# Experts in an order computed on the chip, rows beyond 128 in small fp32 units

## The chip, the cores and the metric

The kernel runs on one core of a Trainium2 chip. The metric is the device time of one execution in microseconds (us), the median of several runs. TensorE (PE in the profile), VectorE (DVE), ScalarE (ACT), GpSimd (POOL) and the queue of SyncE (SP) are the engines that the text names.

## The reference

One inference step of one decoder layer in fp32 for a prompt of 2048 tokens and 8 sample tokens, so 2056 rows of width 1024: a mixer (mLSTM heads and a chunk MLP), then a mixture of experts, then a gated embedding and a norm. What the change touches is the mixture:

```python
g_sel = jnp.argmax(g_prob, axis=-1)                      # one of 4 groups
top_v, top_i = lax.top_k(e_logits, TOP_K_IN_GROUP)       # two of its 8 experts
weights = g_w * jax.nn.softmax(top_v, axis=-1)
expert_idx = (g_sel[:, None] * EXPERTS_PER_GROUP + top_i).astype(jnp.int32)
# rows of an expert, in blocks of 128:
(jax.nn.silu(xb @ w1_l[e]) * (xb @ w3_l[e])) @ w2_l[e]
```

w1 and w3 are 1024 x 512 and w2 is 512 x 1024 for each of the 32 experts, 6.3 MB together. The 4112 choices are spread unevenly over the experts.

## The kernel before

There are four stages, each a block with a barrier at its end. Stages 1 and 2 are the mixer, tile by tile of 128 tokens. In stage 2 the router runs on each tile and GpSimd scatters each row's number into `list_dram`, where every expert has a region of CAP rows. At the end of stage 2 TensorE sums the experts' counts over all partitions (`POS`, L1421), and VectorE turns them into a table `blk` of the first block and the end block of each expert (L1751 to L1764), with at least one block for each. The list of expert 0 is loaded (L1907), its rows are gathered (L1911), its w1 is loaded by `load_first` and split by ScalarE ahead of the barrier.

Stage 3 is the expert stage (L2009 to L2257). All engines run over the experts 0 to 31 in their order, `all_blocks`, and within an expert over its blocks of 128 rows, read from `blk` into registers. The products are made in fp32r with operands split in two parts: hi is the value as fp32r (a ScalarE copy), lo the difference (a VectorE or GpSimd subtraction), and a product is hi x hi, hi x lo and lo x hi.

- TensorE, `block_of` (L2106): 24 products of 512 columns for w1 into bank H1 and 24 for w3 into H3 (L2113 to L2115), 8 transposes of the next block's rows (L2102) and 4 of `hid` (L2121), and 24 products for w2 into two banks (L2132, L2136).
- ScalarE: tanh of H1 (L2174), the copy of the block before's result into `y_sb` and its store (`y_out`, L2163), the hi copies of hid and of x, and once an expert, `after`: the hi copies of the next expert's w3 and w2 and of the w1 after that.
- VectorE: `up` and `hid` (L2217, L2222), the lo parts of hid and x, and five of the six half matrices of lo weights an expert (L2212). GpSimd makes the sixth, the second half of w1 (L2070), in about twice the time.
- GpSimd also loads the next block's list (L2056) and gathers its rows by indirect DMA (L2061).
- SP: `reload` loads each half matrix of the next expert (1 MB) as soon as the raw buffer is free, which is when the lo part has been made. There are three raw buffers, and 4 slots each of w_hi and w_lo, so that a part can be split while the expert before is still in use. SP also copies 16 blocks of filler into the part of `y_dram` that no block writes (L2033).

After the last block VectorE computes for each token and choice its row in `y_dram` (`choices_rows`, L2230), and the weights of the last stage's gate are loaded and split in the same way. Stage 4 gathers two result rows for each token, adds them to h, and makes the gate, the embedding and the norm, tile by tile.

## Time and profile before

| | us |
|---|---|
| median of 3 runs | 2258.27 |
| lowest and highest | 2257.19, 2259.78 |
| the profiled execution | 2255.27 |
| its span, first to last instruction | 2253.7 |
| mean granted TensorE clock of it | 0.977 |

The rows come from one profiled execution. PE is TensorE's products, PEld its weight loads, which overlap them. Times in the rows of the timeline are from the span's start. A product's duration in a row includes its way through the array; the distance between two starts is what a stream of them costs. A true-fp32 product shows as two records, a product in fp32r as one.

### The profile page before, as it was taken

The numbers are of one execution on the slowest core, as the hardware profiler recorded it, in microseconds if no ns is written. First come the engines' busy times: TensorE is split into PE (matmuls) and PEld (weight loads), VectorE is DVE, ScalarE is ACT, GpSimd is POOL, SyncE is SP. The second block draws the span as 40 slices with busy tenths as digits, with TensorE's granted clock in tenths as the row PEclk, the third lists the DMA queues.
The fourth block names the chain that finished last, engine by engine and source line by source line (L and its number), as shares of the span: only waits on it lengthen the run. The fifth ranks groups of instructions, "written<-read, shape, count | busy, mean of one in ns | idle before, by whom it ended". The sixth has DMA issues, their size and how long they took to land. (4 is left out here: it accounts for less than half of the span.)

```text
span 2253.7 us, 34056 instructions
## 1 busy us (share of the span) xinstructions
PE 2149.3 (95%) x10539; PEld 1773.2 (79%) x10540; DVE 1430.6 (63%) x2866; ACT 971.0 (43%) x1569; POOL 581.7 (26%) x595
## 2 busy tenths in 40 slices
PE   6999999999899999994889999999999999899998
PEld 5878888888788888884778888888888878767775
DVE  5788888888566665564536465665566566846554
ACT  4433344444432222222435465665556465623332
POOL 1121111111244333332121223233332132233332
PEclk9999999999999999996999999999999999999999
DMA  6111110132534333324787677898787778943441
GB/s 231 60 38 66 65 60 37 65 112 92 187 107 136 121 121 117 103 91 147 292 309 256 219 266 289 292 363 289 283 294 260 289 290 305 334 169 125 158 141 49
DMA packets 160333, 407.13 MB, mean 181 GB/s; under 512 B 18835, under 2 KB 22347, under 8 KB 160014
## 3 DMA queue, kind: packets, MB, share of 16 engines
q1 hardware_dynamic: 138518, 337.17, 42.0%
q0 software_dynamic: 14560, 43.11, 5.8%
q10 hardware_dynamic: 7200, 26.22, 2.9%
q8 instruction: 23, 0.38, 0.1%
q14 instruction: 32, 0.26, 0.0%
HBM read 330.12 MB, written 84.82 MB: 184 GB/s over the span
## 5 line engine op out<-in xcount | busy, mean ns | idle before, releaser
L234 PE MATMUL bank<-w_hi,mix_x 128*128 128x512 f32 x816 | 333.3, 408 | 9.9 <-DMA mix_x<-xT_dram 4.0
L236 PE MATMUL bank<-w_hi,mix_x 128*128 128x512 f32 x816 | 323.8, 397 | 0.0
L235 PE MATMUL bank<-w_lo,mix_x 128*128 128x512 f32 x816 | 322.9, 396 | 0.0
L2113 PE MATMUL bank<-w_hi,x_hi 128*128 128x512 f32 x784 | 307.6, 392 | 8.1 <-POOL w_lo L2070 4.6
L2212 DVE TENSOR_TENSOR w_lo<-raw,w_hi 128x2048 fp32r<-128x2048 f32 x130 | 292.6, 2311 | 34.8 <-ACT w_hi L2149 34.7
L2115 PE MATMUL bank<-w_hi,x_lo 128*128 128x512 f32 x784 | 307.1, 392 | 0.0
L2114 PE MATMUL bank<-w_lo,x_hi 128*128 128x512 f32 x784 | 307.1, 392 | 0.0
L2149 ACT ACTIVATE w_hi<-raw 128x2048 fp32r<-128x2048 f32 x130 | 238.8, 1925 | 4.8 <-DMA raw<-in_w 4.8
L2070 POOL TENSOR_TENSOR w_lo<-shared,w_hi 128x2048 fp32r<-128x2048 f32 x31 | 157.2, 5071 | 231.7 <-DMA shared<-hn_dram,entry 131.9
L234 PEld LDWEIGHTS bank<-w_hi,mix_x 128*128 128x128 f32 x816 | 156.7, 192 | 42.0 <-issue 5.1
L236 PEld LDWEIGHTS bank<-w_hi,mix_x 128*128 128x128 f32 x816 | 156.3, 192 | 34.7
L235 PEld LDWEIGHTS bank<-w_lo,mix_x 128*128 128x128 f32 x816 | 156.7, 192 | 29.9
L2113 PEld LDWEIGHTS bank<-w_hi,x_hi 128*128 128x128 f32 x784 | 148.5, 189 | 39.9 <-POOL w_lo L2070 5.0
L2115 PEld LDWEIGHTS bank<-w_hi,x_lo 128*128 128x128 f32 x784 | 148.4, 189 | 31.0
L2114 PEld LDWEIGHTS bank<-w_lo,x_hi 128*128 128x128 f32 x784 | 148.5, 189 | 30.9
L248 POOL TENSOR_SCALAR stat<-stat 128x4 f32<-128x4 f32 (+3 forms) x67 | 13.4, 200 | 514.2 <-ACT junk L716 271.2
L2061 POOL DMA_INDIRECT shared<-hn_dram,entry x49 | 68.2, 1392 | 282.9 <-DMA entry<-list_dram 139.3
L2149 ACT ACTIVATE hidT_hi<-bank 128x128 fp32r<-128x128 f32 x98 | 37.6, 384 | 226.3 <-PE bank L2121 226.3
L2217 DVE SCALAR_TENSOR_TENSOR up<-tanh_h,bank 128x512 f32<-128x512 f32 x49 | 33.5, 684 | 157.4 <-ACT tanh_h L2174 157.4
L2132 PE MATMUL bank<-w_hi,hidT_hi 128*128 128x512 f32 x392 | 126.6, 404 | 0.0
L2132 PE MATMUL bank<-w_lo,hidT_hi 128*128 128x512 f32 x392 | 122.3, 393 | 0.0
L2149 ACT ACTIVATE w_hi<-shared 128x2048 fp32r<-128x2048 f32 x64 | 119.7, 1921 | 4.7 <-DMA shared<-in_w 3.9
(316 smaller groups left out, 4222.1 us busy)
## 6 DMA issues: line engine op xcount, KB each, us to landing
raw<-in_w SPq DMA_DIRECT2D x128, 1024.0 KB, 8.5
shared<-in_w SPq DMA_DIRECT2D x64, 1024.0 KB, 8.6
y_dram<-y_sb ACTq DMA_DIRECT2D x50, 512.0 KB, 6.9
xT_dram<-mix_x SPq DMA_DIRECT2D x34, 512.0 KB, 3.5
mix_x<-xT_dram SPq DMA_DIRECT2D x34, 512.0 KB, 4.5
shared<-in_w_in SPq DMA_DIRECT2D x24, 512.0 KB, 6.5
small<-in_x_prompt SPq DMA_DIRECT2D x16, 512.0 KB
xr_sb<-in_x_prompt SPq DMA_DIRECT2D x16, 512.0 KB
```

The lines of the kernel that those rows point to most:

```text
L234: pe.matmul(bank[:, :], x_hi[:, k, :], wh[:, k, :], start=(k == 0), stop=False)
L235: pe.matmul(bank[:, :], x_hi[:, k, :], wl[:, k, :], start=False, stop=False)
L236: ins = pe.matmul(bank[:, :], x_lo[:, k, :], wh[:, k, :], start=False, stop=(k == KD - 1))
L2061: pool.indirect_dma_start(out=rows_in[:, :], out_offset=None, in_=hn_dram[0:NT * P + NS, :], in_offset=bass.IndirectOffsetOnAxis(ap=entry[ ...
L2070: pool.tensor_tensor(w_lo[slot(j, 0)][:, cols], raw[0][:, cols], w_hi[slot(j, 0)][:, cols].bitcast(F32), ALU.subtract).then_inc(w1_lo, 1)
L2113: pe.matmul(bank[:, :], x_hi[:, k, :], wh[:, k, :], start=(k == 0), stop=False)
L2114: pe.matmul(bank[:, :], x_hi[:, k, :], wl[:, k, :], start=False, stop=False)
L2115: ins = pe.matmul(bank[:, :], x_lo[:, k, :], wh[:, k, :], start=False, stop=(k == KD - 1))
L2132: pe.matmul(Y[n][:, :], hidT_hi[:, k, :], col(w, k, n), start=(k == 0 and w is wh), stop=False)
L2149: return act.activation(out, in_, ACT.Copy)
L2212: dve.tensor_tensor(w_lo[slot(j, m)][:, cols], raw[m][:, cols], w_hi[slot(j, m)][:, cols].bitcast(F32), ALU.subtract).then_inc(w1_lo if is ...
L2217: STT(up[:, :], tanh_h[:, :], 1.0, H1[:, :], ALU.add, ALU.mult).then_inc(up_done, 1)
```

## The change

**Order.** At the end of stage 2 VectorE computes, beyond the counts, for each expert the number of units of 32 rows that it has beyond its first 128 rows, and a place in a sequence of steps: one with no unit, then pairs of one expert with units and one without, and at the end what is left. The table `blk` has three rows: first unit, end unit and expert of each step. Three bounds in `ends_of` say where the pairs begin, where they end and which is the last step. List, rows and w1 of the first expert can be fetched only when its number is known (after 30 of the 43 small steps), and w1 is split behind the barrier.

**Steps.** Every step runs the first 128 rows of its expert as before. An expert with more rows has these in units of 32 rows. A unit of the expert of step s + 1 runs in step s, from the raw weights of step s + 1 in true fp32, which have been loaded but not yet used up: 32 products of 256 columns (w1 and w3 side by side) and 16 for w2, four neighbours of which write the four quarters of the partitions. Between the two groups, each unit runs the first half of w2's product of step s.

**Buffers.** w_hi and w_lo have 3 slots in place of 4. TensorE waits for the next step's split w1 between the two halves of w2's product. The next w1 is loaded when the units are done (`tails_done`).

**Other parts.** The filler of `y_dram` is 12 copies of 368 rows in stage 1, in place of 16 copies of 128 rows in stage 3. `choices_rows` is in the last step, ahead of `up`, with another formula for the row. The result rows of a unit are stored as 32 rows.

The core of the diff:

```diff
+                            TS(blk[:, 0, 0:NE], POS, float(TAIL - 1 - P), None, ALU.add).then_inc(rank_steps, 1)
...
+                            TT(placed[0], at.unsqueeze(1).to_broadcast([P, TABLE, NE]), number[:, :].unsqueeze(2).to_broadcast([P, TABLE, NE]), ALU.is_equal).then_inc(rank_steps, 1)
...
                             sp_.wait_ge(log_mm, NTILE)
-                            load_first(1)
+                            sp_.wait_ge(rank_steps, 30)
+                            expert = sp_.value_load(blk[0:1, 2, 0:1], min_val=0, max_val=NE - 1)
+                            for c in range(2):
+                                load_first(expert, c)
...
-                            for c in range(2):
-                                act.wait_ge(raw_loaded[0][c], 16)
-                                copy(w_hi[0][:, c * RH:(c + 1) * RH], shared[:, c * RH:(c + 1) * RH]).then_inc(hi_ready, 1)
...
+                def each_step(eng, ends, step):
+                    pairs, tails, last = ends
+                    step(0, False)
+                    with eng.Fori(1, pairs) as s:
+                        step(s, False)
+                    with eng.Fori(pairs, tails, 2) as s:
+                        step(s, True)
+                        step(s + 1, False)
+                    with eng.Fori(tails, last) as s:
+                        step(s, True)
+                    step(last, False, True)
...
+                        def step(s, more):
+                            x1 = expert_at(sp_, s + 1)
+                            wait_lo(sp_, s, 1, 1)
+                            load(x1, 1, raw_loaded[1])
+                            wait_lo(sp_, s, 2, 1)
+                            load(x1, 2, raw_loaded[2])
+                            x2 = expert_at(sp_, s + 2) if more else None
+                            sp_.wait_ge(tails_done, s + 1)
...
+                        def down(n, k):
+                            wh, wl, cols = w_down(w_hi), w_down(w_lo), slice(n * 512, (n + 1) * 512)
+                            begun = pe.matmul(Y[n][:, :], hidT_hi[:, k, :], wh[:, k, cols], start=(k == 0), stop=False)
+                            pe.matmul(Y[n][:, :], hidT_hi[:, k, :], wl[:, k, cols], start=False, stop=False)
+                            return begun, pe.matmul(Y[n][:, :], hidT_lo[:, k, :], wh[:, k, cols], start=False, stop=(k == KF - 1))
...
+                        def tail(i, s):
+                            for m in range(2):
+                                for c in range(2):
+                                    pe.wait_ge(*raw_in(s + 1, m, c))
+                            pe.wait_ge(t_x_in, i + 1)
+                            w13 = raw13[:, :].rearrange("p (m k n) -> p m k n", m=2, k=KD)
+                            for k in range(KD):
+                                for q in range(TILES):
+                                    ins = pe.matmul(UP_T[q * TAIL:(q + 1) * TAIL, :].rearrange("p (m n) -> p m n", m=2), xT_t[:, k, :],
+                                                    w13[:, :, k, q * P:(q + 1) * P], start=(k == 0), stop=(k == KD - 1))
+                            ins.then_inc(t_up_mm, 1)
+                            ready_down(s)
+                            for k in range(KF):
+                                down(0, k)
+                            pe.wait_ge(t_rows, 16 * i + 32)
+                            pe.wait_ge(t_hid, i + 1)
+                            pe.transpose(HID_T, hid_t[:, :], ident[:, :]).then_inc(t_hid_tp, 1)
+                            tail_transposes()
+                            for c in range(2):
+                                pe.wait_ge(*raw_in(s + 1, 2, c))
+                            pe.wait_ge(t_y_in, i + 1)
+                            pe.wait_ge(t_hidT_in, i + 1)
...
+                            for k in range(KF):
+                                for q in range(TILES):
+                                    ins = pe.matmul(DOWN_T[q * TAIL:(q + 1) * TAIL, :], hidT_t[:, k * TAIL:(k + 1) * TAIL],
+                                                    w2[:, k, q * width:(q + 1) * width], start=(k == 0), stop=(k == KF - 1))
+                            ins.then_inc(t_down_mm, 1)
...
+                            if tailed:
+                                with pe.Fori(first, end) as i:
+                                    tail(i, s)
+                            else:
+                                ready_down(s)
                                 for k in range(KF):
-                                    ins = pe.matmul(Y[n][:, :], hidT_lo[:, k, :], col(wh, k, n), start=False, stop=(k == KF - 1))
-                                ins.then_inc(done, 1)
+                                    down(0, k)
+                            if not last:
+                                for c in range(2):
+                                    wait_lo(pe, s + 1, 0, c)
+                            for k in range(KF):
+                                begun, ended = down(1, k)
+                                if k == 0:
+                                    begun.then_inc(tails_done, 1)
```

ScalarE's and VectorE's order in a step: x copies and lo, then w3, then (ScalarE) the result of the step before, w2, its store, tanh, the next step's w1, hid, the next x, and the units.

## Rows read from the trace of the kernel before

**Rows 1.** The page: busy time of TensorE, share of the span, instructions.

```profile
PE 2149.3 (95%) x10539; PEld 1773.2 (79%) x10540; DVE 1430.6 (63%) x2866; ACT 971.0 (43%) x1569; POOL 581.7 (26%) x595
```

**Rows 2.** Windows: the mixer, then parts and whole of the expert stage.

```profile
core 0: us, PE busy (x) PEld busy (x) DVE busy (x) ACT busy (x) POOL busy (x), PEclk, DMA share, GB/s
0.00:1050.00 1050.00, 994.91 (x5293) 847.39 (x5294) 734.08 (x2198) 374.65 (x839) 238.71 (x313) 0.97 0.30 100
1061.00:1166.00 105.00, 92.30 (x398) 75.19 (x399) 52.24 (x48) 48.10 (x51) 20.34 (x11) 0.91 0.87 326
1166.00:1966.00 800.00, 793.34 (x3720) 653.25 (x3718) 481.04 (x461) 461.99 (x489) 230.96 (x117) 1.00 0.79 287
1061.00:1966.00 905.00, 885.64 (x4116) 728.45 (x4116) 533.28 (x509) 510.08 (x539) 251.29 (x128) 0.99 0.80 291
```

**Rows 3.** Lines: first w1/w3 product, last w2 product (count, ns, first and last start).

```profile
L2113 PE MATMUL bank<-w_hi,x_hi x784: 389/389/792, 1061.4 to 1957.3; 128*128 128x512 f32 x196
L2136 PE MATMUL bank<-w_hi,hidT_lo x392: 388/389/390, 1080.5 to 1965.6; 128*128 128x512 f32 x196
```

**Rows 4.** Timeline of TensorE (start, duration, count): products and transposes.

```profile
1086.65 0.39 PE L2114 MATMUL bank<-w_lo,x_hi 128*128 128x512 f32 x1
1086.88 0.39 PE L2115 MATMUL bank<-w_hi,x_lo 128*128 128x512 f32 x1
...
1094.13 0.60 PE L2102 MATMUL bank<-ident,shared 128*128 128x128 f32 x4
...
1238.35 0.62 PE L2132 MATMUL bank<-w_hi,hidT_hi 128*128 128x512 f32 x2
1238.80 0.63 PE L2132 MATMUL bank<-w_lo,hidT_hi 128*128 128x512 f32 x2
```

**Rows 5.** Timeline of VectorE: `hid` of two neighbouring blocks.

```profile
1236.14 0.75 DVE L2222 SCALAR_TENSOR_TENSOR hid<-up,bank 128x128 f32<-128x128 f32 x2 [1.44 <-PE bank L2115]
1254.05 0.75 DVE L2222 SCALAR_TENSOR_TENSOR hid<-up,bank 128x128 f32<-128x128 f32 x2 [4.19 <-PE bank L2115]
```

**Rows 6.** Waits in the expert stage: TensorE for GpSimd's half of w1.

```profile
PE bank L2113 <- POOL w_lo L2070: 4.6, 1, 4.6
```

**Rows 7.** True-fp32 products: records of L2399, then L2399 and L1360 in the timeline.

```profile
L2399 PE MATMUL bank<-shared,hz x136: 590/592/1192, 1973.1 to 2232.3; 128*128 128x512 f32 x128, 128*8 128x512 f32 x8
...
2074.80 3.59 PE L2399 MATMUL bank<-shared,hz 128*128 128x512 f32 x8
...
1034.06 1.13 PE L1360 MATMUL bank<-small,shared 128*8 128x36 f32 x16 [0.37 <-ACT shared L1426]
```

**Rows 8.** Timeline from the last rank product to the expert stage.

```profile
1041.20 0.64 PE L1421 MATMUL bank<-seen,ones 128*128 128x32 f32 x2 [1.43 <-DVE idx_last L1665]
1041.87 0.19 DVE L1751 TENSOR_SCALAR blk<-bank 128x32 int32<-128x32 f32 x1 [0.73 <-PE bank L1421]
1042.10 0.18 DVE L1753 TENSOR_SCALAR blk<-blk 128x32 int32<-128x32 int32 x1
...
1045.99 0.63 POOL L1907 DMA_DIRECT2D entry<-list_dram  x1 [1.70 <-DMA list_dram<-tok_last,idx_last]
1049.22 1.05 POOL L1911 DMA_INDIRECT shared<-hn_dram,entry  x1 [2.61 <-DMA entry<-list_dram]
...
1055.43 4.49 DVE L2212 TENSOR_TENSOR w_lo<-shared,w_hi 128x2048 fp32r<-128x2048 f32 x2 [12.05 <-PEq L1198]
```

**Rows 9.** Timeline of the last block's end: row numbers (DVE), y store (ACT queue).

```profile
1962.94 1.29 DVE L2235 TENSOR_TENSOR hot<-rowbase,ecap 128x1088 f32<-128x1088 f32 x1
1966.77 0.34 ACTq L2170 DMA_DIRECT2D y_dram<-y_sb  x1
```

**Rows 10.** Timeline: ScalarE's and VectorE's splits of 4 half matrices, GpSimd's of one.

```profile
1256.87 7.34 ACT L2149 ACTIVATE w_hi<-raw 128x2048 fp32r<-128x2048 f32 x4
1258.83 8.90 DVE L2212 TENSOR_TENSOR w_lo<-raw,w_hi 128x2048 fp32r<-128x2048 f32 x4 [1.00 <-ACT w_hi L2149]
L2070 POOL TENSOR_TENSOR w_lo<-shared,w_hi x31: 4557/4611/6407, 1100.3 to 1939.7; 128x2048 fp32r<-128x2048 f32 x31
```

**Rows 11.** DMA issues to landing, us: weights, filler, and list and gather (min/median/max).

```profile
raw<-in_w SPq DMA_DIRECT2D x128, 1024.0 KB, 8.5
y_dram<-hn_dram SPq DMA_DIRECT2D x16, 512.0 KB, 15.0
DMA to landing us min/median/max: 2.4/4.8/15.1
DMA to landing us min/median/max: 4.1/6.7/15.1
```

More of the change, by code:

```diff
@@ L2090, in _, with shift @@
-                        hold(pool, rows_loaded, 16)
-                        with pool.Fori(0, NE // SLOTS - 1) as quad:
-                            for j in range(SLOTS):
-                                expert(quad * SLOTS + j, j)
-                        for j in range(SLOTS):
-                            expert(NE - SLOTS + j, j)
+                        def shift(bits):
+                            return nc.s_assert_within(bits, 0, 17, skip_runtime_bounds_check_because="none or all of the bits, by a flag of 0 or 1")
@@ new lines, in step @@
+                        def step(s, tailed, last=False, apart=2):
+                            if last:
+                                return
+                            if tailed:
+                                mine, after = expert_at(pool, s + 1), expert_at(pool, s + apart)
+                                first, end = span(pool, s + 1)
+                            gather(s + 1)
+                            if tailed:
+                                with pool.Fori(first, end) as i:
+                                    left = nc.s_assert_within(end - i - 1, 0, 127, skip_runtime_bounds_check_because="i runs from first to end - 1")
+                                    more = (left + 127) >> 7
+                                    here = nc.s_assert_within(mine * CAP + (i + 1 - first) * TAIL + P, P, (NE + 1) * CAP,
+                                                              skip_runtime_bounds_check_because="a unit is one of its expert's")
+                                    gather_tail(i + 1, (here >> shift(17 - 17 * more)) + ((after * CAP + P) >> shift(17 * more)))
+                            load_list(s + 2)
+                            split_w1(s + 1)
@@ L2187, in _ @@
+                            if tailed:
+                                with act.Fori(first, end) as i:
+                                    tail(i, s)
+                        act.sem_inc(t_stored, 16)
+                        act.sem_inc(t_y_in, 1)
                         act.sem_inc(y_stored, 16)
+                        ends = bounds(act)
                         x_halves(0)
-                        split(0, 0, 1)
-                        split(0, 0, 2)
-                        all_blocks(act, block_of, after)
@@ L2192, in _ @@
-                        total = count_all(act)
-                        y_out(total)
-                        act.wait_ge(y_stored, total * 16 + 32)
+                        split(0, 0)
+                        each_step(act, ends, step)
+                        split(ends[2] + 1, 1)
+                        y_halves(ends[2] + 1)
+                        y_out(ends[2] + 1)
+                        total = entry_of(act, 1, ends[2], MAXT, 1)
+                        act.wait_ge(t_stored, total * 16 + 16)
@@ L2263, in program @@
+                        ends = bounds(dve)
+                        split(0, 0, (0,))
+                        split(0, 0, (1,), w1_lo)
+                        each_step(dve, ends, step)
+                        split(ends[2] + 1, 1, signal=gate_lo)
         with ExitStack() as late:
```

572 lines of the change are left out of this document (350 added, 222 removed).

## The prediction

> **What bounds the kernel now.** I read the page's busy line first: TensorE is busy 95% of the span [rows 1], so what is worth anything is TensorE time, or idle time of TensorE. The windows over the expert stage come next: it runs from the first w1 product at 1061.4 us to the last w2 product at about 1966.0 us, 904.6 us [rows 2, 3], with the DMA engines 80% busy and 291 GB/s moved. The form counts give the work: 784 products of L2113 are 49 blocks of 16 [rows 3]. In the timeline fp32r products start 0.226 us apart (0.227 in w2) and four transposes take 0.60 us [rows 4]: 48 x 0.226 + 12 x 0.1 + 24 x 0.227 = 17.5 us, and the distance between two blocks' `hid` is 17.91 us [rows 5]. So 49 blocks are 877 us and the stage has 27.5 us of stalls and half clock; the first 105 us hold most of them (clock 0.91, PE busy 92.3) [rows 2], one being a 4.6 us wait for the half of w1 that GpSimd splits [rows 6].
>
> **What the change does to the work.** Evaluating the reference's router on its inputs gives the rows of each expert: 4112 choices, 32 experts with 73 to 194 rows, which round up to the 49 blocks of the trace. 17 experts have more than 128 rows and their rests make 25 units of 32 (ten experts with one, six with two, one with three). That gives 32 steps: steps 0 and 1 without a unit, then 12 pairs (units, none), steps 26 to 30 with units, step 31 without. The terms:
>
> (a) *17 blocks gone*: 17 x 17.9 = -304.3 us on the bounding engine. The old stalls, -27.5, go too and are put in anew below.
>
> (b) *25 units*. One is 32 + 16 = 48 true-fp32 products of 256 columns, each writing 32 partitions, with four neighbours going to the four different quarters of the partitions. No operation like this is in the trace. The nearest: a true-fp32 product shows as two records (136 of L2399 for 68 products), and eight records of 512 columns in 3.59 us start 0.43 us apart [rows 7], so one 256-column record streams for about 0.214 us and a product for 0.43. The cheapest fp32 records, 36 columns with 8 stationary columns, start 0.06 us apart [rows 7]; that is the floor of issue. If four quarters work side by side, a record costs the larger of 0.214/4 and 0.06 us: 96 x 0.06 = 5.8 us a unit. If nothing overlaps it is 48 x 0.43 = 20.6 us. These are the two bounds, and they are far apart. To either come 9 small transposes at 0.1 [rows 4] and four handovers (units to down, to transposes, to down, back) for which I put 0.2 each, since a block of two or three handovers loses 0.4 us in all (17.9 against 17.5): +1.7. I take the lower end, U = 7.5 us, because the products of one group write different partitions and read nothing of each other, but it is the choice on which all hangs: 25 x 7.5 = +187.5.
>
> The Trainium skill, "TensorE: Matmul & The Clock Gate" (Part 3, row/col tiling), speaks for it: small-M products in distinct column groups run concurrently, three of them measured 2.38 times faster than in sequence. By 2.38 a unit's products would take 20.6/2.38 = 8.7 us and the sum would be some 70 us higher, an estimate from that page; no run here shows it yet.
>
> (c) *The first half of w2's product is repeated by each unit* as a filler behind the unit's w1/w3 product (it restarts the accumulation, so only the last counts): 8 units beyond an expert's first x 12 x 0.228 = +21.9. The filler, 2.7 us, covers the chain tanh, two small VectorE operations, about 1.5 us; without it that chain would cost 25 x 1.5.
>
> (d) *The start*. After the last rank product at 1041.2 VectorE does 8 small steps; the entry list is fetched at 1046.0, the gather issued at 1049.2, the stage entered at 1055.4, the first product starts at 1061.4 [rows 8, 3]. Now the first expert must be known before its list or its w1 is fetched: 30 steps, of them 14 dependent rounds at 0.22 and 10 others at 0.1 (4.1 us), three over 1152 elements at 1.3 (the nearest, 1088 elements, takes 1.29 [rows 9]), so 1050.3 instead of 1043.4, and with a register load 1051.4 for the list: everything up to the stage's entry 5.5 us later. w1's split, until now done ahead of the barrier, comes behind it: x copies, ACT 2 x 1.9, VectorE 2 x 2.3, x_lo 1.3 bring the first product to about 1072.4: +11 (between +7 and +15).
>
> (e) *New stalls*. The 4 slots for split weights become 3, with one raw buffer for each matrix, and TensorE now waits for the next step's w1 between the two halves of w2's product. In a step that follows units, counted from the last unit's end: ScalarE copies and stores y (0.8), splits w3 (3.7, to 4.5), copies Y (5.6), splits w2 (9.3), issues, tanh (10.4), splits w1 (14.1), GpSimd's half ends 4.6 to 6.4 us later at 18.8 to 20.6 [rows 10]. TensorE has 2.7 + 10.9 + 1.6 + 2.7 = 17.9 us of work until it asks. Stall about 2 us in 12 steps, 24 us; in steps with units the same split hides behind the units. Steps 0 and 1: 4. In 17 steps with units the products ask for raw w3 at 12.5 us, its load goes out when VectorE has freed the buffer at about 3.8 and takes 8.5 [rows 11]: about 1 us each, 17. The row numbers of the choices (4.4 us on VectorE, until now behind the last block, beside the y store [rows 9]) stand in the last step ahead of `up`: 3.5. Half clock at the start as now: 8 (a clock of 0.91 over the first 105 us [rows 2] is 19 us at 1.2 GHz, some 9 lost). Sum +56.5 (20 to 100).
>
> (f) *At nothing*: 12 copies of 1.5 MB in the mixer's loop on SP's queue, in place of 16 of 0.5 MB that stood in the first expert stretch with 15.0 us to landing [rows 11]. Behind each, the next load of x is issued a tile later, and that part moves few bytes (100 GB/s, 30% [rows 2]). If the cover failed it would be up to 12 x 8 us. The second batch of dependent rank steps (to about 1057) ends before the stage is entered. The gather of units: list 4.8, issue 1, landing 6.7 [rows 11], behind at least one unit with its filler; only the expert with three units waits, 2 us. The block's end still waits for the last y store, and the stage after it is unchanged.
>
> Sum: -304.3 - 27.5 + 187.5 + 21.9 + 11 + 56.5 = -54.9 us. The profiled execution took 2255.3 (span 2253.7), the median is 2258.3; I set the difference against the median: **2203 us**.
>
> In general the result is 2258.3 - 242.4 + 25 U: it is no gain at U = 9.7, that is when one of the 48 products costs 0.167 us.
>
> **Rivals.** *Order (slower).* A product's two records go to the same quarter. If records start strictly in program order, the second has to wait out the first, and only the second of one product and the first of the next overlap: 0.218 us a product, 48 x 0.218 + 1.7 = 12.1 us a unit, 25 x 12.1 = 302.5, total +60: **2318**. It decides from 0.167 us a product on. For it: all neighbouring products here start in order and none passes another; two records a product [rows 7]. Against: nothing in these rows has two quarters in it. The same page of the Trainium skill (Part 3, what overlaps) states that MATMULs are monotone in start and end, strict FIFO, and this is what it would do here; the trace agrees as far as it goes, with starts in order 0.43 us apart.
>
> *No overlap at all (slower).* 48 x 0.43 + 1.7 = 22.3 us a unit: +315, **2573**. For it: no product of the trace overlaps another's streaming.
>
> *Transfers.* Units read the raw weights, so their buffers stay occupied and the DMA engines idle in them. The stage moves 32 x 6.3 MB of weights, 20 MB of gathers and 20 of y, 241 MB in the 839 us that I forecast, 288 GB/s, about what it moves now, but in fewer stretches; the best stretch of rows 2 is 326 GB/s at 87%. If w3 and w2 land 3 us after they are wanted in each of the 17 steps with units, the gain is nearly gone: **2253**. Against: pairs give the queues some 46 us for 14.8 MB.
>
> *Not what it says*: a wrong count of units or empty steps would show in the counts; 3 steps too many would be +54, 2257.
>
> **Chances.** Forecast 0.46; order 0.28; transfers 0.10; no overlap 0.10; count 0.02; better than forecast by over 25 us, if stalls vanish, 0.04. A measurement of this kernel can tell about 0.2%, 4.5 us, from no change. Faster 0.53 (forecast, better, part of transfers), same 0.07, slower 0.40. The range from 2180 to 2335 takes in the forecast with its bounds, transfers and order, and leaves out the rest. The forecast's own range is 2180 to 2240.
>
> **What would show it.** The unit's w1/w3 line: 64 records a unit, 3.8 us if four work side by side, 7 if two, 13.7 if none; w2's half of that. 25 executions of tanh on 128 columns, 32 on 512. The first product near 1072. PE idle on the GpSimd split line in every other step, about 2 us. Idle of PE ahead of the unit's product on a DMA of raw weights shows the transfers. The clock in the stage stays at 2.4 GHz (granted 1.00 in the window from 1166 to 1966 [rows 2]); if it were granted half in units, a unit would double. The prediction is wrong above all if a unit's product costs more than 0.167 us.

## The result: about half a per cent slower, where 2.4% faster was forecast

| | us |
|---|---|
| before, median of 8 runs | 2260.23 (2257.19 to 2267.26) |
| after, median of 8 runs | 2275.39 (2270.69 to 2279.43) |
| ratio after/before | 1.006, 95% interval 1.0044 to 1.0075 |
| the profiled execution of after, its span | 2279.43, 2277.8 |
| forecast | 2203, range 2180 to 2335 |

The sign is wrong. The profiled execution is the longest of the eight, 4 us over their median. The page of after, busy line and four of the costliest groups (busy, mean ns, idle time before and what ended it):

```profile
PE 2070.6 (91%) x11832; PEld 1641.3 (72%) x11833; DVE 1449.4 (64%) x2831; ACT 954.0 (42%) x1547; POOL 616.6 (27%) x612
...
L2426 DVE TENSOR_TENSOR w_lo<-raw,w_hi 128x2048 fp32r<-128x2048 f32 x99 | 276.1, 2817 | 123.5 <-ACT w_hi L2327 123.4
...
L2255 PE MATMUL bank<-raw,xT_t 128*32 128x256 f32 x1600 | 116.6, 456 | 54.2 <-DMA raw<-in_w 54.2
L2426 DVE TENSOR_TENSOR w_lo<-shared,w_hi 128x2048 fp32r<-128x2048 f32 x66 | 148.3, 2288 | 26.0 <-ACT w_hi L2327 24.4
L2236 PE MATMUL bank<-w_hi,hidT_hi 128*128 128x512 f32 x288 | 122.1, 424 | 36.1 <-DVE hidT_lo L2470 19.0
```

TensorE lost 79 us of work against [rows 1], as the change promises, and the time went up all the same: from 95% busy it fell to 91%. The lines of the first and the last product of the expert stage, and windows over the stage and over one step of it (columns as in [rows 2]):

```profile
L2284 PE MATMUL bank<-w_hi,x_pair x512: 389/389/795, 1080.7 to 1973.9; 128*128 128x512 f32 x171
L2238 PE MATMUL bank<-w_hi,hidT_lo x288: 387/393/628, 1104.9 to 1989.2; 128*128 128x512 f32 x144
```

```profile
core 0: us, PE busy (x) PEld busy (x) DVE busy (x) ACT busy (x) POOL busy (x), PEclk, DMA share, GB/s
1081.00:1989.00 908.00, 803.30 (x5408) 594.40 (x5408) 542.35 (x440) 490.84 (x515) 284.64 (x143) 0.96 0.75 265
1645.00:1661.00 16.00, 12.80 (x62) 10.36 (x60) 11.61 (x10) 10.28 (x10) 7.47 (x3) 1.00 1.02 351
1661.00:1666.00 5.00, 4.78 (x60) 2.69 (x64) 2.50 (x1) 0.00 (x0) 3.22 (x2) 0.66 0.97 359
1666.00:1672.00 6.00, 6.00 (x65) 3.91 (x57) 1.84 (x4) 0.94 (x3) 0.59 (x1) 1.00 0.15 60
```

The stage takes 908.8 us (1080.7 to 1989.5) against 904.6 before [rows 2, 3]. It holds 105 us in which TensorE is not busy, against 19 before, and a clock of 0.96 against 0.99. What ended TensorE's waits in it (us in total, times, longest), where before had the 4.6 us of [rows 6], 13.7 us for gathers and 3.5 us for `x_lo`:

```profile
PE bank L2255 <- DMA raw<-in_w: 54.2, 17, 4.7
PE bank L2224 <- issue: 25.3, 1, 25.3
PE bank L2236 <- DVE hidT_lo L2470: 19.0, 15, 1.3
PE bank L2236 <- DVE w_lo L2426: 17.1, 13, 1.4
```

The 25.3 us lie ahead of the stage. The other three are new, and the largest is a transfer (each load of `in_w` is a half matrix of weights). Step 20, which has one unit, in TensorE's timeline:

```profile
1657.32 0.49 PE L2301 MATMUL bank<-ident,hid 128*128 128x128 f32 x3
1661.22 5.35 PE L2255 MATMUL bank<-raw,xT_t 128*32 128x256 f32 x64 [3.41 <-DMA raw<-in_w]
1666.50 0.50 PE L2236 MATMUL bank<-w_hi,hidT_hi 128*128 128x512 f32 x1
...
1669.60 0.68 PE L2230 MATMUL bank<-ident,rows_t 32*128 32x32 f32 x8
1670.21 1.93 PE L2273 MATMUL bank<-shared,hidT_t 128*32 128x256 f32 x32
```

TensorE waits 3.41 us for the raw w3 of the next expert, which the unit reads. Then its product takes 5.35 us, in a window in which the granted clock is 0.66 [the windows above]: the level falls to 1.2 GHz during it, behind the wait, and is back at 2.4 GHz from 1666. The DMA engines are the other half of the picture: 1.02 busy at 351 GB/s up to 1661, then 0.15 at 60 GB/s while the unit holds the raw buffers and nothing may be loaded.

**Where the forecast's error lies.** Against its own base (2255.3) the forecast is 2200.4 and the profiled execution is 2279.4, 79 us more. A step is taken from its first w1 product (L2284) to that of the next:

| | forecast, us | measured, us | sum of the difference |
|---|---|---|---|
| first product of the stage | 1072.4 | 1080.7 | +8.3 |
| step 0 | 27.9 | 31.4 | +3.5 |
| 13 steps without units | 19.9 | 21.5 | +20.5 |
| 10 steps with one unit | 26.4 | 29.8 | +34 |
| 6 with two, 1 with three | 36.6, 46.9 | 37.7, 47.3 | +7 |
| the last step | 21.4 | 26.5 | +5 |
| behind the stage | 287.7 | 288.3 | +0.6 |

### The profile page after: what moved, and what is told of

Read it like the earlier page. It is cut to its first block and busy times, and to the rows that moved or that the text cites. A ratio compares the mean times of both kernels' runs of the same rounds, so it can differ in the third digit from the quotient of the medians.

```text
span 2277.8 us, 36186 instructions
## 1 busy us (share of the span) xinstructions
PE 2070.6 (91%) x11832; PEld 1641.3 (72%) x11833; DVE 1449.4 (64%) x2831; ACT 954.0 (42%) x1547; POOL 616.6 (27%) x612
## 5 line engine op out<-in xcount | busy, mean ns | idle before, releaser
L2426 DVE TENSOR_TENSOR w_lo<-raw,w_hi 128x2048 fp32r<-128x2048 f32 x99 | 276.1, 2817 | 123.5 <-ACT w_hi L2327 123.4
L249 PE MATMUL bank<-w_hi,mix_x 128*128 128x512 f32 x816 | 334.1, 409 | 10.2 <-DVE w_lo L232 4.3
L2284 PE MATMUL bank<-w_hi,x_pair 128*128 128x512 f32 x512 | 202.4, 395 | 13.3 <-DVE x_pair L2418 8.7
L2179 POOL TENSOR_TENSOR w_lo<-raw,w_hi 128x2048 fp32r<-128x2048 f32 x31 | 141.3, 4557 | 259.9 <-ACT w_hi L2327 259.8
L2285 PE MATMUL bank<-w_lo,x_pair 128*128 128x512 f32 x512 | 200.3, 391 | 0.0
L2286 PE MATMUL bank<-w_hi,x_pair 128*128 128x512 f32 x512 | 200.2, 391 | 0.0
L2255 PE MATMUL bank<-raw,xT_t 128*32 128x256 f32 x1600 | 116.6, 456 | 54.2 <-DMA raw<-in_w 54.2
L2426 DVE TENSOR_TENSOR w_lo<-shared,w_hi 128x2048 fp32r<-128x2048 f32 x66 | 148.3, 2288 | 26.0 <-ACT w_hi L2327 24.4
L2255 PEld LDWEIGHTS bank<-raw,xT_t 128*32 128x32 f32 x1600 | 60.8, 130 | 104.3 <-issue 83.1
L2284 PEld LDWEIGHTS bank<-w_hi,x_pair 128*128 128x128 f32 x512 | 96.7, 189 | 39.9 <-DVE w_lo L2426 11.0
L2641 PE MATMUL bank<-w_hi,hT_hi 128*128 128x512 f32 x272 | 113.8, 418 | 2.0 <-DVE hT_lo L2714 2.0
L2238 PE MATMUL bank<-w_hi,hidT_lo 128*128 128x512 f32 x288 | 114.8, 399 | 0.0
## 6 DMA issues: line engine op xcount, KB each, us to landing
shared<-in_w SPq DMA_DIRECT2D x66, 1024.0 KB, 10.2
```

The lines of the kernel that those rows point to most:

```text
L249: pe.matmul(bank[:, :], x_hi[:, k, :], wh[:, k, :], start=(k == 0), stop=False)
L2179: pool.tensor_tensor(w_lo[0][:, cols], raw_of(s, 0)[:, cols], w_hi[0][:, cols].bitcast(F32), ALU.subtract).then_inc(w1_lo, 1)
L2255: ins = pe.matmul(UP_T[q * TAIL:(q + 1) * TAIL, :].rearrange("p (m n) -> p m n", m=2), xT_t[:, k, :], w13[:, :, k, q * P:(q + 1) * P], sta ...
L2284: pe.matmul(bank[:, :], x_hi[:, k, :], wh[:, k, :], start=(k == 0), stop=False)
L2285: pe.matmul(bank[:, :], x_hi[:, k, :], wl[:, k, :], start=False, stop=False)
L2286: ins = pe.matmul(bank[:, :], x_lo[:, k, :], wh[:, k, :], start=False, stop=(k == KD - 1))
```

## The experiments

Edits are made to the kernel after. Ratios are against before on the same chip, whose median there was 2259.0 to 2261.5 us. "Step with one unit" and the like are means over steps 1 to 30 of the profiled execution.

**The control** is the kernel after, unchanged.

> The changed kernel as it is, to have its time beside the experiments on one chip. All theories: 2275 us within 5, TensorE's idle time ahead of the units' w1/w3 products about 54 us in 17 waits on raw weights, and these products 5.3 us in the steps where the clock fell, 3.7 where it did not.

2270.6 us, ratio 1.0049 (1.003 to 1.0067). On this chip the wait for raw w3 was 49.8 us in 17 times, the step with one unit 29.1 us. `a1_filled`, `b4_w3_half` and `b1_ahead` ran on the same chip and are read against this.

**Is it the idle time that costs the clock?** `a1_filled` puts twelve products of w2's first half, which the unit repeats anyway, ahead of the wait for raw w3.

```diff
                             if tailed:
+                                ready_down(s)
+                                for k in range(KF):
+                                    down(0, k)
                                 with pe.Fori(first, end) as i:
                                     tail(i, s)
```

> The changed kernel with 12 products that nobody needs (w2's first half, made again later) ahead of the wait for the raw weights in each of the 17 steps with units: 17 x 2.74 = 46.6 us of added work. Theory 1, the weights land late and the idle time costs a second time since the clock falls to 1.2 GHz behind it: the added products stand in the wait, 0.5 us of each wait is left, the clock stays up, 14 x 1.65 = 23 us are saved: about 2252 us, faster than the changed kernel although it does more. Theory 2, only the wait counts and the clock falls for another reason, such as the small products themselves: no change, 2275. Theory 3, TensorE's own work is what the raw weights' buffers wait for, so that all later loads shift by the added work: +47, 2322.

2269.7 us, ratio 1.0037 (1.0023 to 1.0051). Its wait rows, and its unit in step 20:

```profile
PE bank L2236 <- DVE hidT_lo L2473: 40.5, 32, 1.3
```

```profile
1653.04 0.39 PE L2238 MATMUL bank<-w_hi,hidT_lo 128*128 128x512 f32 x1
1653.36 3.66 PE L2255 MATMUL bank<-raw,xT_t 128*32 128x256 f32 x64
```

17 x 2.74 = 46.6 us of work were added and the time did not change, as the second theory had it; the clock did what the first one said. The unit starts at +16.8 us in the step instead of +15.9, without a wait, and takes 3.66 us instead of 5.35. No step with units has a stretch at 1.2 GHz any more (37.5 us of them in the control, 54.6 in after's profile), and the busy time of L2255 is 91.3 us instead of 107.9 in the control and 116.6 in after's profile. So the fall of the clock comes from TensorE standing still ahead of the unit, and its price was 25 us in after's profiled execution and 17 in the control's. It doesn't follow each wait: 14 of the 17 waits had one in after and 10 in the control, with none behind a wait of 3.54 us and one behind 2.15 us. What decides between them is open. The gain was eaten by the filler, which itself has to wait for `hidT_lo` in 17 more steps (40.5 us in 32 times against 19.0 in 15), and by its own length: 46.6 + 21.5 against 49.3 of the wait and 17 of the clock.

**Is the wait one for bandwidth?** `b4_w3_half` loads only the first half of each half of w3 (0.5 MB instead of 1 MB).

```diff
-                        def load(x, m, sems):
+                        def load(x, m, sems, part=1):
...
-                            load(x1, 1, raw_loaded[1])
+                            load(x1, 1, raw_loaded[1], 2)
```

> The changed kernel with each step's load of w3 cut to half its bytes (1 MB in place of 2 MB; the other half of w3 keeps the values of an expert before, so the outputs are not the reference's). Theory 1, bandwidth: the queues are busy without a gap from the release of w1 to the landing of w3, so 3 us of transfer less take away the wait of 3.2 us (54 us) and the low clock behind it (23 us): 2200 us, or a little less. Theory 2, the load is issued late, since it waits for VectorE's lo parts, and takes its latency whatever its size: a latency of 8.9 us falls by about 1 us, 17 us in all: 2258.

2208.5 us, ratio 0.9763 (0.9747 to 0.978). Waits, and the first 13 us of step 20 with the unit's product behind them:

```profile
PE bank L2255 <- DMA raw<-in_w: 7.5, 9, 2.4
```

```profile
1604.60:1617.60 13.00, 12.53 (x61) 10.13 (x59) 8.71 (x8) 9.23 (x9) 4.89 (x3) 1.00 1.02 350
1617.60:1621.40 3.80, 3.75 (x65) 2.22 (x66) 3.70 (x2) 1.06 (x4) 3.65 (x2) 1.00 1.00 385
```

The same rate, 350 GB/s at full share, over 13 us instead of 16: 1 MB less is 3 us less, which is 350 GB/s again. The unit starts 0.5 us after TensorE gets to it, and its clock is 1.00. The median is 62 us under the control's, the profiled execution 56 (2209.8 against 2266.0): 42 of them are the wait (49.8 to 7.5) and some 17 the clock (37.5 us at half in the steps with units, now 3.6), while other steps gave a few us back. So the wait is one for bandwidth, and it brings the clock's fall with it.

**Use the repeated products as the cover, and repeat them no more.** `b1_ahead` has w2's first half once, ahead of the units, and takes it out of `tail`.

```diff
                             ins.then_inc(t_up_mm, 1)
-                            ready_down(s)
-                            for k in range(KF):
-                                down(0, k)
                             pe.wait_ge(t_rows, 16 * i + 32)
...
                             if tailed:
+                                ready_down(s)
+                                for k in range(KF):
+                                    down(0, k)
                                 with pe.Fori(first, end) as i:
```

> The changed kernel with w2's first half made once, ahead of the units (so in the wait for the raw weights), and not again in each unit. Theory 1: 8 x 2.74 = 22 us of repeated products go, 17 x 2.74 = 46 us of the wait are used, the clock stays up (-23), and the chain of tanh, up and hid lies open in each unit, 25 x 1.6 = +40: 2224 us. Rival: the open chain leaves TensorE idle in each unit so that the clock falls there, 25 units with a product of 1.65 us more: 2265. If the wait is not covered (theory 3, loads shift with TensorE's work): 2290.

2232.5 us, ratio 0.987 (0.9853 to 0.9886): faster than both kernels. Waits:

```profile
PE bank L2236 <- DVE hidT_lo L2470: 40.4, 32, 1.3
PE bank L2260 <- DVE up L2433: 28.3, 25, 1.1
```

The wait for raw w3 and the half clock are gone from the steps with units (27.2 us with one, 29.1 in the control). In their place stand the wait for `hidT_lo` and the chain from tanh to the unit's `hid` (a part of the tile `up`), 1.1 us a unit, which the repeated products had covered.

**The steps without units.** TensorE there waits for `hidT_lo` (1.3 us) and for the next w1's lo half (1.3 us). `a2_late_wait` asks for the latter, and gives the signal that frees the raw buffers, at the last product of w2's second half instead of the first.

```diff
-                            if not last:
-                                for c in range(2):
-                                    wait_lo(pe, s + 1, 0, c)
+                            at_k = 0 if tailed or last else KF - 1
                             for k in range(KF):
+                                if not last and k == at_k:
+                                    for c in range(2):
+                                        wait_lo(pe, s + 1, 0, c)
                                 begun, ended = down(1, k)
-                                if k == 0:
+                                if k == at_k:
                                     begun.then_inc(tails_done, 1)
```

> The changed kernel, in steps without units alone: the wait for the next step's split w1, and the signal that lets SP load over it, stand before the last of w2's products in place of the first of its second half. 9 products, 2.0 us, come ahead of the wait, which is 1.4 us in 13 steps. Theory 1, TensorE's wait is on the way and its time is free to take: 13 x 1.4 = 18 us less than the changed kernel, 2252. Theory 2, the same signal starts ScalarE's copy of the result and the next load, both now behind the same VectorE operation plus some of the products, and the next step loses what this one gains: 2270, no change.

2279.1 us, ratio 1.0092 (1.0067 to 1.0116): slower. The steps without units fell from 21.5 to 20.1 us, as the edit should bring, and those with one unit rose from 29.8 to 31.1:

```profile
PE bank L2255 <- DMA raw<-in_w: 71.9, 17, 6.2
```

The next w1's load goes out later and stands in front of w3's. What a step without units gains, the pair's next step gives back in the wait for transfers, and more through the clock (71 us at 1.2 GHz). In the kernel after, the pair is bound by its transfers, not by either step's own work.

`a3_hi_first` runs the eight products with the hi part of `hidT` first and the four with the lo part last, in steps without units.

```diff
+                        def down_hi_first(s):
+                            wh, wl, cols = w_down(w_hi), w_down(w_lo), slice(0, 512)
+                            if not first_step(s):
+                                pe.wait_ge(y_in, 2 * s)
+                            for c in range(2):
+                                wait_lo(pe, s, 2, c)
+                            for part, ks in enumerate(K_OF):
+                                pe.wait_ge(hidT_hi_ready, 2 * s + part + 1)
+                                for k in range(*ks):
+                                    pe.matmul(Y[0][:, :], hidT_hi[:, k, :], wh[:, k, cols], start=(k == 0), stop=False)
+                                    pe.matmul(Y[0][:, :], hidT_hi[:, k, :], wl[:, k, cols], start=False, stop=False)
+                            pe.wait_ge(hidT_lo_ready, 2 * s + 2)
+                            for k in range(KF):
+                                pe.matmul(Y[0][:, :], hidT_lo[:, k, :], wh[:, k, cols], start=False, stop=(k == KF - 1))
...
                             else:
-                                ready_down(s)
-                                for k in range(KF):
-                                    down(0, k)
+                                down_hi_first(s)
```

> The changed kernel, in steps without units alone: w2's first half begins with the 8 products that need only hid's hi part, as before the change, and the 4 with its lo part follow, so that the wait for VectorE's lo part (19.0 us in 15 steps) is covered. Theory 1, the wait is on the way: -19, 2251 us. Theory 2, the wait behind it in the same step, for VectorE's split of the next w1, ends at a time that TensorE does not set, and grows by what the first loses: 2270, no change, and that wait rises from 18 to about 37 us.

2260.9 us, ratio 1.0003 (0.9991 to 1.0015). Waits:

```profile
PE bank L2270 <- DMA raw<-in_w: 44.9, 17, 4.5
PE bank L2236 <- DVE w_lo L2439: 34.9, 14, 3.5
```

The wait for `hidT_lo` is gone, and the wait for w1's lo half took its whole time: 17.1 to 34.9 us. Steps without units became no shorter (22.2 against 21.5). The median is still 14 us under after's and 10 under the control's, each on another chip, and no trace explains that. Against after's profile the wait for w3 is shorter and so are step 0 and the last step, some 2 us each, but that was after's longest execution. Here the profiled execution is the longest of ten, 2266.6, and the control's is the shortest of six, 2266.0: these two are equal. What takes 10 us off the median is open.

**Does alternating carry anything?** `b2_order` makes one pair and puts the other steps without units in a row, then those with units.

```diff
-                            TT(at_step[:, 2:3], at_step[:, 1:2], at_step[:, 0:1], ALU.min).then_inc(rank_steps, 1)
+                            TS(at_step[:, 2:3], at_step[:, 1:2], 0.0, 1.0, ALU.mult, ALU.add).then_inc(rank_steps, 1)
```

> The changed kernel with one pair in place of twelve: steps without units first, 14 in a row, then the experts with units in a row. Theory 1, alternating carries the gain, since steps without units are bound by transfers (7.3 MB a step at 350 to 400 GB/s is 18 to 21 us, and the single buffers leave gaps): each step without units takes 2 us more, +28, 2298 us. Theory 2, alternating is worth nothing or costs: a step behind a step without units has all engines ahead (21.2 us as step 1, against 21.8 in the pairs), and the steps with units in a row take 28.8 and 36.0 us for one and two units, against 29.3 and 37.0 in the pairs: -15, 2255.

2263.0 us, ratio 1.0021 (1.0006 to 1.0037): not slower than the alternating order. The wait for raw w3 is 45.4 us in 17 times, in a row or not. A step with a unit leads to its own wait, whatever comes ahead of it; the likely reason is that the load of w3 that it waits for is issued within it, which no run tests by itself.

**Does the overlap of the quarters depend on neighbours?** `b3_q_outer` exchanges the two loops of a unit's products, so that all of one quarter's come in a row.

```diff
-                            for k in range(KD):
-                                for q in range(TILES):
+                            for q in range(TILES):
+                                for k in range(KD):
                                     ins = pe.matmul(UP_T
```

> The changed kernel with the two loops of a unit's products exchanged: all products of one quarter of the partitions, then the next quarter. The work and its result are the same. Theory 1, quarters run side by side only where neighbours in the program go to different quarters, and products start in program order: 64 records at 0.216 us are 13.8 us in place of 3.7, and 6.9 in place of 1.9 for w2, so 25 x 15.1 = 377 us more, 2648 us. Theory 2, the array has a queue for each quarter and takes them out of order: no change, 2270.

2532.4 us, ratio 1.1211 (1.1178 to 1.1245). In the timeline:

```profile
1650.31 11.50 PE L2255 MATMUL bank<-raw,xT_t 128*32 128x256 f32 x64 [3.12 <-DMA raw<-in_w]
1684.10 4.59 PE L2273 MATMUL bank<-shared,hidT_t 128*32 128x256 f32 x32
```

11.50 and 4.59 us against 3.65 and 1.93: (7.85 + 2.66) x 25 = 263 us, near the difference of the medians, 2532 - 2275 = 257 (two executions, on another chip). The starts of the 64 records are 0.216 us apart within a quarter, and only around a change of the quarter do two run side by side, which is why the time lies under the 2648 us of the first theory; in after four records start 0.0067 us apart, and the next four 0.216 us later. The records of one quarter are serial and four quarters run side by side if neighbours go to different ones.

**Put together.** `c2_ahead_hi` is `b1_ahead` with `down_hi_first(s)` in all 32 steps; `c3_ahead_hi_order` is that with the edit of `b2_order`; `c1_all` is that of `c2_ahead_hi` with the edit of `a2_late_wait`; `c4_hi_in_tailed` has `down_hi_first` in the 17 steps with units only.

```diff
+                            down_hi_first(s)
                             if tailed:
                                 with pe.Fori(first, end) as i:
                                     tail(i, s)
-                            else:
-                                ready_down(s)
-                                for k in range(KF):
-                                    down(0, k)
```

> As b1_ahead (w2's first half once, ahead of the units), and with its eight products of the hi half of hidT first and the four of the lo half last, in all 32 steps. In b1_ahead TensorE waited for hidT_lo 40.4 us in 32 steps, 1.3 us each. Theory 1 (in steps with units TensorE's own row of work is now the bound): the 17 steps with units lose their 1.3 us each, 22 us, the 15 without lose nothing, as in a3_hi_first, where the wait for the next w1's lo half took its place: 2232 - 22 = 2210 us. Theory 2 (the raw w3 is the next thing late in steps with units too: b1_ahead only just covers it): the wait for the load comes back by what the products leave earlier, and the time stays near 2232 us, with some half clock. Beside it: the wait for hidT_lo goes to near 0 in both.

> As c2_ahead_hi, with the experts with units last and in a row, but for one pair, instead of alternating (the order of b2_order). In after this order cost about 0.3% less or nothing, because its steps with units were bound by the load of raw w3 in either order. Theory 1 (with the first half of w2 ahead, the load is covered in every order): within 0.5% of c2_ahead_hi. Theory 2 (alternation now pays, since the step without units lets the next one's loads run ahead): wait for raw w3 in the row of steps with units, some 17 x 1 us, so 0.7% over c2_ahead_hi.

> As c2_ahead_hi, and in steps without units the wait for the next w1's lo half (and the signal that frees the raw buffers) stands ahead of the last product of w2's second half instead of the first, as in a2_late_wait. Theory 1 (the raw buffers bind: in a2_late_wait the later signal lengthened the steps with units by 1.7 us while those without became 1.5 us shorter): with about 1 to 2 us of slack won by w2's first half ahead of the units, the steps without units gain 1.5 us each (15 of them, 22 us) and those with units give back half or more: 2200 to 2215 us. Theory 2 (slack enough): 2188 us.

> As c2_ahead_hi, but with the products of the hi half first only in the 17 steps with units; the 15 without keep the order of b1_ahead. In c2_ahead_hi the steps with units were 1.1 us shorter than in b1_ahead (26.0 against 27.15), but those without were 0.5 to 1.6 us longer (22.6 to 23.3 against 21.3 to 21.8): TensorE then waits up to 3.8 us in one piece for the lo half of the next w1, and the clock halves for 3.4 us in 8 of them; with the wait for hidT_lo (1.3 us) in between it stayed at full speed. Theory 1 (the idle time in one piece costs the clock): 2232 - 17 x 1.1 = 2213 us, no half clock in the steps without units. Theory 2 (the splits of the next w1 are late in both, since the units free the raw buffers earlier): 2221 us, as c2_ahead_hi.

| | us | ratio and interval | step without, with one unit |
|---|---|---|---|
| `c2_ahead_hi` | 2221.5 | 0.9829 (0.981 to 0.9849) | 22.7, 26.4 |
| `c3_ahead_hi_order` | 2217.7 | 0.9818 (0.9802 to 0.9835) | 21.7, 26.8 |
| `c1_all` | 2217.6 | 0.9817 (0.98 to 0.9833) | 20.3, 28.3 |
| `c4_hi_in_tailed` | 2217.5 | 0.9808 (0.979 to 0.9827) | 21.5, 26.8 |

All four are faster than before by 1.7 to 1.9%, and their intervals overlap, so the time doesn't rank them. `c2_ahead_hi` and `c4_hi_in_tailed` lie between the times of their two theories, `c1_all` just above its first, and order is worth nothing again. The traces do tell them apart. In `c2_ahead_hi` the hi products run at once and TensorE then waits in one piece; in `c4_hi_in_tailed` the same time comes in two pieces with 3.0 us of products between. First `c2_ahead_hi`, timeline and windows at the end of step 21:

```profile
1656.67 1.07 PE L2260 MATMUL bank<-w_hi,hidT_lo 128*128 128x512 f32 x4
1660.25 0.49 PE L2236 MATMUL bank<-w_hi,hidT_hi 128*128 128x512 f32 x1 [2.51 <-DVE w_lo L2435]
```

```profile
1660.20:1664.40 4.20, 4.15 (x12) 3.26 (x13) 4.20 (x4) 0.60 (x1) 1.34 (x2) 0.67 0.67 189
```

Then `c4_hi_in_tailed`, the same step:

```profile
1647.27 0.47 PE L2236 MATMUL bank<-w_hi,hidT_hi 128*128 128x512 f32 x1 [1.26 <-DVE hidT_lo L2483]
1651.65 0.49 PE L2236 MATMUL bank<-w_hi,hidT_hi 128*128 128x512 f32 x1 [1.39 <-DVE w_lo L2439]
```

```profile
1651.60:1654.50 2.90, 2.85 (x12) 2.36 (x13) 2.90 (x3) 0.60 (x1) 1.34 (x2) 1.00 0.55 120
```

Behind 2.51 us in one piece the granted clock is 0.67 and twelve products take 4.2 us; behind 1.39 us it is 1.00 and they take 2.9. Over the 13 middle steps without units that is 31 us at 1.2 GHz against none. `c1_all` shows the coupling of `a2_late_wait` once more: -2.4 us a step without units, +1.9 with.

## Why the prediction was wrong, point by point

(a) *17 blocks gone* and the counts: right. 512 products of L2284 are 32 steps, 1600 of L2255 are 25 units.

(b) *25 units at 7.5 us*: right, and somewhat dear. 64 records in 3.65 us at full clock (forecast 3.8 for four side by side) and 32 in 1.93. The 0.06 us that the forecast took for the floor of issue isn't one, since neighbours started 0.0067 us apart; its number came out near by luck, as 0.216/4 is 0.054. At full clock a second unit starts 9.0 us after the first, of which 2.74 are repeated products, so U is 6.3, and 25 x 1.2 = 30 us less than forecast. *Order* and *No overlap* fall with the 3.65 us; `b3_q_outer` shows that *Order*'s premise, serial records in one quarter, holds, but not its conclusion: the second record of a product doesn't have to follow the first at once, as the four firsts start before it. The Trainium skill, "TensorE: Matmul & The Clock Gate" (Part 3), gives 2.38 for three tiles; here four quarters gave 64 x 0.216/3.65 = 3.8.

(c) *Repeated products*, 21.9: right in size (2.74 each, 8 of them). The chain that they cover is 1.1 us, not 1.5, by `b1_ahead`. So each repeat costs 2.74 and covers 1.1. The place is the point: behind the unit these products cover 1.1 us, ahead of it 3.2 and the clock.

(d) *The start*, +11 forecast, +19.3 measured. The timeline from the last rank product on:

```profile
1044.13 0.64 PE L1437 MATMUL bank<-seen,ones 128*128 128x32 f32 x2 [1.43 <-DVE idx_last L1677]
...
1054.46 1.05 SPq L1228 DMA_DIRECT2D shared<-in_w  x2
...
1055.04 0.63 POOL L1980 DMA_DIRECT2D entry<-list_dram  x1 [7.80 <-DVE step_of L1816]
...
1061.62 1.05 POOL L1984 DMA_INDIRECT shared<-hn_dram,entry  x1 [5.96 <-DMA entry<-list_dram]
1070.05 1.96 PE L2224 MATMUL bank<-ident,shared 128*128 128x128 f32 x8 [25.28 <-issue]
...
1080.71 0.80 PE L2284 MATMUL bank<-w_hi,x_pair 128*128 128x512 f32 x1 [8.70 <-DVE x_pair L2418]
```

The rank product is 2.9 us later than in [rows 8]. Whether the change does that, with the filler copies now in the mixer, can't be told: in the profiled executions of after and its variants this product starts between 1040.5 and 1046.0, and before has only one. From it to the list's issue are 10.9 us, forecast 10.2: right. What was missed is that w1's 2 MB now go out 0.6 us ahead of the list: the list landed 5.7 us after its issue, before 2.4, and it was 6.6 us to the gather's issue, before 3.2 [rows 8]. The list was taken at the price that it had alone. From the gather's issue to the stage it is 8.4 against 6.2, though the gather itself landed after 4.4 us in both; the 2.2 us behind its landing are open. From the stage's entry to the first product it is 10.7 us, forecast 11.5. 2.9 + 0.7 + 3.4 + 2.2 - 0.8 = 8.4.

(e) *New stalls*, 56.5 forecast. This is the step that failed, in four terms, two of them with no term in the sum.
- *w3 late, 17 x 1*: 54.2 us, 3.2 each. SP's queue around step 20, which begins at 1645.2:

```profile
1643.03 6.44 SPq L2106 DMA_DIRECT2D raw<-in_w  x4
1652.37 0.89 SPq L2106 DMA_DIRECT2D shared<-in_w  x2
```

The first row holds w1 and w3, whose halves are issued at 1648.0 and 1648.6, about 3 us into the step (forecast 3.8); the second is w2. w3's landing was put at 8.5 us, the median of [rows 11]. The two issues of w3 and their landing:

```profile
raw<-in_w SPq DMA_DIRECT2D x2, 1024.0 KB, 11.3
```

The later half landed at 1661.0, 12.4 us after its issue. The median of [rows 11] is one over loads of the whole stage, with 5.1 to 15.6 us in it. Here w1, w3 and w2, 2 MB each, go out within 10 us, and the engines are at 1.02 for 16 us. The mean over the stage, 288 GB/s, was held against the best stretch, 326, where the question was what has to land by 12.6 us into the step. `b4_w3_half` shows it.
- *The clock*: no term at all in the steps with units; 25 us. I wrote that the clock stays at 2.4 GHz, though the same list had a wait ahead of each unit. `a1_filled` shows the cause, and `b4_w3_half` and `b1_ahead` agree.
- *`hidT_lo`*: no term; 19.0 us in 15 steps. Before, the products with the hi part stood first and the lo part, made meanwhile, came later [rows 4]; now every product of w2 waits for both (L2245). It could be read in the diff, yet `a3_hi_first` shows that its removal alone is worth nothing there, since the next wait takes its time.
- *The next w1, 12 x 2 us*: 17.1 in 13. The size is near, but what was waited for is VectorE's half, not GpSimd's. VectorE and GpSimd, and what TensorE waited for, in step 21:

```profile
1689.23 4.47 DVE L2426 TENSOR_TENSOR w_lo<-raw,w_hi 128x2048 fp32r<-128x2048 f32 x1
```

```profile
1686.99 4.57 POOL L2179 TENSOR_TENSOR w_lo<-raw,w_hi 128x2048 fp32r<-128x2048 f32 x1 [18.18 <-ACT w_hi L2327]
```

```profile
1693.84 0.49 PE L2236 MATMUL bank<-w_hi,hidT_hi 128*128 128x512 f32 x1 [1.37 <-DVE w_lo L2426]
```

VectorE's split takes 4.47 us instead of the usual 2.29. GpSimd's had begun 2.24 us earlier and ran for 2.33 us of it, about the excess of 2.18. The Trainium skill, "SBUF — State Buffer" (SBUF: two separate sides), says that a VectorE operation with two SBUF inputs and a GpSimd operation that reads SBUF exclude each other, the later one blocked until the first is done; this row agrees, to 0.15 us. I costed the two engines' splits as parallel.

Steps 0 and last: 3.5 and 5.1 us over. Step 0 has 15.2 us at 1.2 GHz (about 8 lost, as forecast), and its 3.5 us are not resolved further; in the last step `hid` is transposed from +15.9 us on, behind a wait of 4.2 us, where 3.5 were forecast, with 6.8 us at 1.2 GHz around it.

Not all is put down to a line. A step without units takes 21.5 us, and 17.9 with the two waits of 1.3 are 20.5. Of the 13 us that this leaves over 13 steps, at most 4.5 are a wait for VectorE's half of w3 (L2284, 10 times); the rest is open.

(f) *Nothing*: right as far as seen. The part behind the stage is unchanged, and the filler copies show no wait.

*The rival Transfers* was the right mechanism and even the right size, 3 us in each of 17 steps, and got a chance of 0.10. Its own argument, buffers occupied and DMA engines idle in the units, is the line with 0.15; against it stood only a mean over a pair. Its 2253 lacks the clock's 25 us, `hidT_lo` and the start, and takes a unit 1.2 us too dear.

## What to carry to other kernels

When work is taken off the bounding engine, ask of every transfer in a step when it is issued, what else is issued within its flight, and by when it must land; a median landing time and a mean rate, both over the whole stage, hide the answer. Work that must be done anyway belongs ahead of the wait that it can cover, and a short wait costs more than its length if the clock falls behind it. An edit of one step of a chain of steps that share buffers is to be judged over the pair: what one gained here, its neighbour gave back.

## What was not expected of the hardware

- True-fp32 records of 256 columns that write four different quarters of the partitions start 0.0067 us apart, four every 0.216 us, so that 64 take 3.65 us; in order of quarters they take 11.5.
- Behind waits of 2.51 and 3.41 us the granted clock was 0.67 and 0.66 and a unit's product took 5.35 us instead of 3.66; behind 1.26 and 1.39 us with 3.0 us of products between them it stayed at 1.00. So waits of a few us inside a busy stage can cost more than themselves. A fall isn't certain: it came behind 14 of 17 such waits in one execution of after and 10 of 17 in another.
- VectorE's split of 128x2048 took 2.29 us where no split of GpSimd's ran. In after's trace 24 of them began while one did, and each took longer by the length of the overlap less 0.14 us, up to 5.78 us in all: the two engines' splits ran one after the other, not side by side.
